# The last two token blocks of a PEER layer: both whole expert tables multiplied on TensorE in place of gathers

## Chip, core and metric

The kernel runs on one core of a Trainium2 chip. The metric is the device time of one execution in microseconds (us). The 16 DMA engines of the core, the GpSimd queue that issues gathers (POOL), SyncE's queue of plain transfers (SP), TensorE (PE), VectorE (DVE) and ScalarE (ACT) all take part.

## What is computed

One residual layer on 1024 tokens of width 1024: a token mixer (convolution branch, stick-breaking attention branch, gates, output projection, LayerNorm) and then a channel mixer, PEER, in blocks of 128 tokens. Only PEER is touched by the change:

```python
def block(xb):                                   # 128 tokens
    q = (xb @ w_q).reshape(128, 8, 2, 128)
    s1, s2 = einsum('thd,hkd->thk', q[:, :, 0], k1), einsum(..., q[:, :, 1], k2)
    v1, i1 = top_k(s1, 16);  v2, i2 = top_k(s2, 16)
    top_s, pos = top_k(v1[..., :, None] + v2[..., None, :], 16)   # of 256 pairs
    idx = i1 * 128 + i2 at pos                   # one of 16384 experts
    gate = softmax(top_s)
    act = gelu(einsum('td,thkd->thk', xb, expert_u[idx]))
    return einsum('thk,thkd->td', gate * act, expert_v[idx])
x = layer_norm(alpha * x + PEER(x))
```

All is float32. A token of a head picks 16 experts, so a block of 128 tokens needs 8 x 16 = 128 pairs of rows (u, v) per token.

## The kernel before, in words

The token mixer of the second half of the sequence (four blocks) is done first. Then one long run of **turns** does PEER: one turn is one head of one block, 8 blocks x 8 heads = 64 turns (`TURNS`), and a turn has 8 **steps** (`STEPS`). A step handles two of the 16 picked experts per token. Blocks 4 to 7 of the turns are the first half of the sequence; their token mixer (late convolution, late attention, late mixing) is spread over the steps of turns 1 to 31 by hand, in `beside(t, g)`.

In a step (turn t, step g) this happens:
- POOL gathers, for each of the two experts, 128 rows of the joined table `uv` (8 KB each: u and v) into one of `RING` = 8 slots (L727; a slot is free when `experts` of four steps earlier is done).
- DVE takes the dot product of x1 with the u half (`dots`, L2033), then a part of the top-k of a later turn (`pick`), then the part of `beside`.
- ACT does the gelu, the product with the gate and two small diagonal matrices (L1480, L1482, L1489).
- PE multiplies the diagonals with the v half, 16 matmuls of 32x32 by 512 columns (`experts`, L1002), in PSUM banks 0 to 3 (4 to 7 for odd late blocks, `y_bank`).

Every engine runs its own list in the order of the steps, so what an engine waits for in a step also holds up what it has to do in the next. The scores of the late blocks for one head ("slab") are made in turns 30 to 38 (`slab_in_turn`); the last slab is scored in turn 38. At the end of a block `merge`, `y_out` and `finish` normalise it and SP stores it.

A float32 matmul stands in the trace as two instructions. The three matmuls of `split_products` (L256 to L258) are the other way that this kernel multiplies: each operand is cut in a rounded fp32r part (made by ACT) and a rest (made by DVE), and each of the three products is one instruction.

Of the kernel before, what the change touches and what calls it, by code (L numbers as in the profile page):

```python
# [29 lines left out]
P = 128  # L30
# [49 lines left out]

def wait_alone(eng, sem, value, started):


    value = eng.to_reg(value)
    eng.wait_ge(started, 1)
    eng.wait_ge(sem, value)
# [5 lines left out]
TURNS = NB * PH  # L92
# [89 lines left out]
def build(nc, xT_d, x_d, w_proj_d, w_v_d, w_mix_d, w_out_d, slabs_d, uv_d, cols_d, bv_d,  # L182
          b_out_d, ln1_g_d, ln1_b_d, ln2_g_d, ln2_b_d, out_d):
    ctx = ExitStack()
    with ctx:  # L185
# [22 lines left out]
        x_lo_bytes = overlay("x_lo_bytes", 160, 176, F32R)  # L208
        ctx.enter_context(nc.sbuf_tensor("arenas", [P, HIGH * KB], F32))
# [113 lines left out]

        def small(name, shape, dt=F32):
            return ctx.enter_context(nc.sbuf_tensor(name, [P] + shape, dt))
# [19 lines left out]
        iota_i = small("iota_i", [TOPK], mybir.dt.int32)  # L345
        top_s = small("top_s", [TOPK])
# [131 lines left out]

        block = ctx.enter_context(nc.Block())
# [10 lines left out]
        def y_bank(pb):  # L490
            return 4 if pb > BLK and pb % 2 == 1 else 0
# [17 lines left out]
        def _(sp_eng):  # L509
# [164 lines left out]
            for pb in range(BLK, NB - 1):  # L674
                store_out(pb)
            for half in range(2):
                hs = slice(half * HALF, (half + 1) * HALF)
                sp_eng.wait_ge(out_ready, NB + half)
                sp_eng.dma_start(out_d[row_of(NB - 1):row_of(NB - 1) + P, hs], pre2[:, hs]).then_inc(stored, 16)
            sp_eng.wait_ge(stored, 16 * (NB + 1))  # L680
# [3 lines left out]
        def _(pool):  # L684
# [7 lines left out]
            pool.memset(quad_eye, 0.0).then_inc(pool_step, 1)  # L692
            pool.iota(iota_i[:, :], pattern=[[1, TOPK]], base=0, channel_multiplier=0).then_inc(consts, 1)
# [40 lines left out]
        def _(pe):  # L734
# [272 lines left out]
            def banks_free(pb):  # L1007
                if pb <= BLK and pb >= 1:
                    pe.wait_ge(y_read, pb)
                if pb == BLK + 1:  # L1010
                    pe.wait_ge(score_ready, len(SLABS))
                if pb > BLK + 1:
                    pe.wait_ge(y_read, pb - 1)
# [211 lines left out]

            def select(t, g):
# [30 lines left out]
            for t in range(TURNS):  # L1257
                for g in range(STEPS):
                    if t % PH == 0 and 1 <= t // PH <= BLK and g == 0:
                        merge(t // PH - 1)  # L1260
                    if t % PH == 0 and t // PH > BLK and g == 1:
                        merge(t // PH - 1)
# [18 lines left out]
        def _(act):  # L1281
# [342 lines left out]

            def select(t, g):
# [51 lines left out]
            for t in range(TURNS):  # L1677
                act.wait_ge(gates_ready, t + 1)
                steps = Steps(act, gelu_step, t * TOPK)
                for g in range(STEPS):  # L1680
                    if t % PH == 0 and 1 <= t // PH <= BLK and g == 0:
                        odd_out(t // PH - 1)
# [8 lines left out]
                    if t % PH == 0 and t // PH > BLK and g == 0:  # L1691
                        odd_out(t // PH - 1)
# [4 lines left out]
                    for n in rows_at(t * STEPS + g):  # L1697
                        spread_out(n)
                    if t == 0 and g in (1, 6):
                        std1(2 + g // 4)  # L1700
                assert steps.n == TOPK
            odd_out(NB - 1)
            finish_std(NB - 1)
# [3 lines left out]
        def _(dve):  # L1707
# [249 lines left out]
            dve.wait_ge(consts, 6)  # L1957
            nc.vector.tensor_copy(iota16[:, :], iota_i[:, :]).then_inc(iota_ready, 1)
# [86 lines left out]
            def finish(pb, part):  # L2045
# [8 lines left out]
                if part == 3 and pb + 1 < NB:  # L2054
                    norm_scale(pre2, pre2, ln2_b_bc).then_inc(out_ready, 1)
                if part == 3 and pb + 1 == NB:
                    for half in range(2):
                        hs = slice(half * HALF, (half + 1) * HALF)
                        norm_scale(pre2[:, hs], pre2[:, hs], ln2_b_bc[:, hs]).then_inc(out_ready, 1)
# [142 lines left out]
            next_steps = Steps(dve, topk_step, FIRST_STEPS)  # L2202
            for t in range(TURNS):
                steps, next_steps = next_steps, Steps(dve, topk_step, FIRST_STEPS + (t + 1) * TOPK_STEPS)
                for g in range(STEPS):
                    dots(t, g)
                    if t % PH == 0 and t >= 1 and g == (1 if t // PH > BLK else 0):
# [17 lines left out]
                    beside(t, g)  # L2225
                assert t + 1 == TURNS or steps.n == TOPK_STEPS
            y_out(NB - 1)
            for part in range(4):
                finish(NB - 1, part)
# [57 lines left out]
```

## Time and profile before

| | us |
|---|---|
| median of 3 runs | 3086.72 (3085.66 to 3087.18) |
| the profiled execution, span | 3085.0 |
| PE busy | 2081.4 (67%) |
| DVE busy | 2314.1 (75%) |
| ACT busy | 1153.7 (37%) |
| POOL busy | 1339.0 (43%) |
| moved by DMA | 1172.07 MB, of it 1073.81 MB by the gathers' queue |

The page gives the span in 40 slices of 77 us: tenths of an engine's busy time, the TensorE clock granted (in tenths of 2.4 GHz), the mean busy share of the 16 DMA engines and the GB/s moved. A wait is given as idle time of the engine ahead of a group of instructions, with who ended it. The profiled span is 1.7 us under the median.

### The profile page before, as it was taken

The page shows a single profiled execution, that of the slowest core. Times are in us where ns is not written, and L with a number is a line of the kernel's source. Part 1 is how long each engine was busy: PE and PEld are TensorE (multiplying, and loading weights), DVE is VectorE, ACT ScalarE, POOL GpSimd, SP SyncE. Part 2 cuts the span into 40 slices and gives each one's busy share as a digit, 9 for nine tenths or more (in the row PEclk, how much of TensorE's full clock was granted, in tenths as well). Part 3 has the DMA queues.
Part 4 walks back from the last instruction along what each step waited for, and adds up shares of the span by engine and source line. Part 5 has one row for each costly group of instructions (what it writes and reads, how often), then busy time and mean ns, then how long its engine had stood idle before and what let it go on. Part 6 is the DMA issues. An engine that isn't in the chain of part 4 may idle for free. (4 is left out here: it accounts for less than half of the span.)

```text
span 3085.0 us, 54203 instructions
## 1 busy us (share of the span) xinstructions
PE 2081.4 (67%) x20660; PEld 830.9 (27%) x20660; DVE 2314.1 (75%) x4890; ACT 1153.7 (37%) x3376; POOL 1339.0 (43%) x1175
## 2 busy tenths in 40 slices
PE   9999878787987777678889767654344434443443
PEld 7777433232323333323323222210000000000000
DVE  7965678999789898967668766667776767677764
ACT  3353243333445455534334343333333333333222
POOL 0000244444445555633434444445555555555553
PEclk9999989888987877789989888875555555555555
DMA  4113799999999999999999999999999999999997
GB/s 163 60 64 137 275 413 405 419 416 409 415 421 417 419 417 420 417 421 421 419 420 410 420 421 421 419 419 419 418 419 418 418 420 419 417 417 419 417 419 303
DMA packets 167847, 1172.07 MB, mean 380 GB/s; under 512 B 18357, under 2 KB 18485, under 8 KB 31034
## 3 DMA queue, kind: packets, MB, share of 16 engines
q0 software_dynamic: 147456, 1073.81, 84.1%
q1 hardware_dynamic: 20154, 95.01, 7.9%
q8 instruction: 160, 2.62, 0.3%
q14 instruction: 77, 0.63, 0.1%
HBM read 1164.55 MB, written 4.19 MB: 379 GB/s over the span
## 5 line engine op out<-in xcount | busy, mean ns | idle before, releaser
L727 POOL DMA_INDIRECT arena_high<-uv_dram,idx_now x1024 | 1273.4, 1244 | 1381.9 <-PE ps L1002 1196.2
L2033 DVE SCALAR_TENSOR_TENSOR arena_high<-arena_low,arena_high 128x1024 f32<-128x1024 f32 x1024 | 1242.2, 1224 | 581.1 <-DMA arena_high<-uv_dram,idx_now 572.3
L1002 PE MATMUL ps<-arena_high 32*32 32x512 f32 x16384 | 820.5, 835 | 937.3 <-ACT arena_high L1489 933.3
L1480 ACT ACTIVATE gcol<-hcol 128x2 f32<-128x2 f32 x512 | 104.0, 203 | 1581.6 <-DVE arena_high L2033 1581.3
L1002 PEld LDWEIGHTS ps<-arena_high 32*32 32x32 f32 x16384 | 136.6, 119 | 1483.0 <-ACT arena_high L1489 1402.9
L1489 ACT ACTIVATE arena_high<-arena_high,wcol 128x32 f32<-128x32 f32 x1024 | 272.9, 313 | 16.7
L963 PE MATMUL ps<-arena_low 128*128 128x512 f32 (+1 forms) x512 | 253.2, 637 | 0.2 <-issue 0.2
L1482 ACT ACTIVATE wcol<-gcol,arena_high 128x1 f32<-128x1 f32 x1024 | 245.6, 287 | 16.9
L722 POOL CAST idx_now<-arena_high 128x8 uint32<-128x8 f32 x128 | 62.4, 488 | 209.1 <-DVE arena_high L2019 208.6
L963 PEld LDWEIGHTS ps<-arena_low 128*128 128x128 f32 x512 | 101.9, 213 | 168.8 <-issue 159.2
L1141 PE MATMUL ps<-arena_low 128*128 128x512 f32 x256 | 126.0, 638 | 0.0
L256 PE MATMUL ps<-x_hi_bytes,w_hi_bytes 128*128 128x512 f32 x256 | 104.1, 407 | 7.2 <-DVE x_lo_bytes L1720 7.2
L1480 ACT ACT_TABLE_LOAD x79 | 101.4, 1283 | 6.1 <-DVE arena_high L2033 4.8
L257 PE MATMUL ps<-x_lo_bytes,w_hi_bytes 128*128 128x512 f32 x256 | 101.4, 396 | 0.0
L258 PE MATMUL ps<-x_hi_bytes,w_bytes 128*128 128x512 f32 x256 | 101.2, 395 | 0.0
L1738 DVE SCALAR_TENSOR_TENSOR arena_low<-arena_low,cols 128x512 f32<-128x512 f32 x120 | 90.0, 750 | 2.8
L2033 DVE DVE_READ_ACCUMULATOR arena_high<-arena_low,arena_high 128x1 f32 x1024 | 84.3, 82 | 0.0
L1474 ACT ACT_TABLE_LOAD x64 | 82.1, 1283 | 1.1
L1970 DVE MAX8 arena_high<-arena_high 128x8 f32<-128x128 f32 x256 | 74.2, 290 | 6.1 <-ACT arena_high L1670 5.0
L1125 PE MATMUL ps<-arena_low 128*64 128x128 f32 x416 | 72.3, 343 | 1.2 <-ACT arena_low L1562 1.2
L1971 DVE FIND_INDEX8 top_i<-arena_high 128x8 uint32<-128x128 f32 x256 | 72.8, 284 | 0.0
L1125 PEld LDWEIGHTS ps<-arena_low 128*64 128x64 f32 x416 | 63.4, 180 | 29.2 <-issue 18.0
(207 smaller groups left out, 2546.9 us busy)
## 6 DMA issues: line engine op xcount, KB each, us to landing
arena_low<-slabs_dram SPq DMA_DIRECT2D x20, 1152.0 KB, 10.0
arena_high<-uv_dram,idx_now POOLq DMA_INDIRECT x1024, 12.5
arena_low<-w_mix_dram SPq DMA_DIRECT2D x8, 1536.0 KB, 11.5
arena_high<-w_proj_dram SPq DMA_DIRECT2D x16, 512.0 KB, 3.2
arena_high<-w_mix_dram SPq DMA_DIRECT2D x8, 1024.0 KB, 5.0
arena_low<-w_proj_dram SPq DMA_DIRECT2D x16, 512.0 KB, 11.7
arena_high<-w_mix_dram SPq DMA_DIRECT2D x8, 512.0 KB, 7.0
arena_high<-w_out_dram SPq DMA_DIRECT2D x2, 2048.0 KB, 9.6
```

The source lines that it names most:

```text
L256: nc.tensor.matmul(out, w_hi, x_hi, start=first, stop=False)
L257: nc.tensor.matmul(out, w_hi, x_lo, start=False, stop=False)
L258: return nc.tensor.matmul(out, w_lo, x_hi, start=False, stop=last)
L727: pool.indirect_dma_start(out=ring[:, s % RING, :], out_offset=None, in_=uv_d, in_offset=bass.IndirectOffsetOnAxis(ap=idx_now[:, s:s + 1], ...
L963: last = nc.tensor.matmul(ps[:, 4 + half, j0 * P:j1 * P], w[:, k, half * P:(half + 1) * P], x1T[:, j0:j1, k, :], start=(k == 0), stop=(k = ...
L1002: last = nc.tensor.matmul(ps[out:out + QUAD, y_bank(t // PH) + turn, :], diag[rows, s % DIAGS, :], ring[rows, s % RING, cs], start=fresh, ...
L1125: last = nc.tensor.matmul(ps[r, 7, b * P:(b + 1) * P], v_block(b + m)[:, p * P + hd * DH:p * P + (hd + 1) * DH], kq_late[:, hd, m, :], sta ...
L1141: last = nc.tensor.matmul(ps[:, 4 + g, :], w_mix_late[m % 2][:, o:o + P], xT_late[:, k, :], start=(k == 0), stop=(k == KD - 1))
L1480: steps.link(nc.scalar.activation(gcol[:, s0:s0 + 2], hcol[:, s0:s0 + 2], ACT.Gelu))
L1482: last = nc.scalar.activation(wcol[:, s:s + 1], gcol[:, s:s + 1], ACT.Copy, scale=gates[:, t % (BLK * PH), s:s + 1])
L1489: nc.scalar.activation(diag[:, s % DIAGS, :], quad_eye, ACT.Copy, scale=wcol[:, s:s + 1]).then_inc(diag_ready, 1)
L2033: last = nc.vector.scalar_tensor_tensor(out=ring[:, s % RING, 0:D], in0=x1[c][:, j, :], scalar=1.0, in1=ring[:, s % RING, 0:D], op0=ALU.mu ...
```

## The change

`DENSE` = 2: the last two blocks (6 and 7) leave the turns, `TURNS` is 48. Their PEER is done as dense products with all 16384 experts, beside the steps of turns 39 to 47 (`U0` = 39 x 8 is the first step, 72 steps up to the last):

1. **Picks.** From turn 32 on, one part of a pick of the two blocks per step (`dense_pick`, 16 picks of 5 parts, 80 steps) on DVE, its exponential on ACT. They leave, per token and head, both key numbers and the gate in `picks`.
2. **First table, 41 steps.** u is given transposed, as 128 tiles of 128 experts x 1024 (`ut`). SP loads each (512 KB, 8 slots), PE multiplies it with the 256 tokens (`u_tile`, 8 float32 matmuls of 128x128 by 256 columns), ACT takes the gelu of two tiles at a time (`dense_act`) and SP stores the result in DRAM (`act_d`, 16 chunks of 1 MB).
3. **Gates spread, 16 of these steps** (from the 25th). For groups of four tokens DVE makes one-hot matrices from `picks` (`hot_group`, 8 instructions of 128x128), PE multiplies them (`g_group`, 4 float32 matmuls of 128 columns): the 128 x 128 gates of each token. ACT copies, SP stores (`g_d`, 16 MB in all).
4. **Second table, 31 steps.** SP loads a chunk of gates (1 MB, read in pieces of 512 B) and of activations (1 MB) for 8 tiles and the tiles of v (512 KB, 4 slots). DVE multiplies the chunk (128x2048), ACT rounds it, DVE makes the rest. Of each v tile ACT makes the rounded part, DVE the rest, and PE does `v_tile`: 2 blocks x 2 halves x 3 = 12 matmuls of 512 columns in banks 4 to 7.
5. **End.** `dense_finish` normalises the two blocks one after the other, after the last gathered block.

The merge of all blocks is in banks 0 to 3 (`y_bank` is 0). The diff, cut:

```diff
+DENSE = 2
+GB = NB - DENSE
+TURNS = GB * PH
...
+U0 = 39 * 8
+U_STEPS, V_STEPS = 41, 31
+PICK0 = 32 * 8
+PICK_PARTS = 5
+NT = NKEY
+CH = 8
+GROUPS = DENSE * P // 4
+G_STEP0 = 24
+def u_first(s):
+    return NT * s // U_STEPS
+def v_first(v):
+    return NT * v // V_STEPS
+def w_step(c):
+    return U_STEPS + max(v for v in range(V_STEPS) if v_first(v) <= c * CH) - 1
...
 @block.sync
+            def load_u(n):
+                if n == 0:
+                    sp_eng.wait_ge(score_psum, len(SLABS))
+                if n >= 8:
+                    wait_again(sp_eng, u_used, n - 7)
+                sp_eng.dma_start(u_slot[n % 8].rearrange("p a b -> p (a b)"), ut_d[n, :, :]).then_inc(u_in[n % 8].sem, 16)
+            def load_v(n):
+                if n < 4:
+                    wait_again(sp_eng, u_used, NT - 7 + n)
+                else:
+                    wait_again(sp_eng, v_used, n - 3)
+                sp_eng.dma_start(v_raw[n % 4], uv_d[n * P:(n + 1) * P, D:2 * D]).then_inc(v_in[n % 4].sem, 16)
+            def load_chunk(c):
+                if c == 0:
+                    for i in range(2):
+                        wait_again(sp_eng, act_stored[i], 16 * NT // CH // 2)
+                        wait_again(sp_eng, g_stored[i], 16 * 16 // 2)
+                if c >= 2:
+                    wait_again(sp_eng, v_used, CH * (c - 1))
+                src = g_d[:, :, c * CH * 16:(c + 1) * CH * 16].rearrange("a p b -> p a b")
+                sp_eng.dma_start(g_in[c % 2], src).then_inc(chunk_in[c % 2].sem, 16)
+                sp_eng.dma_start(act_in[c % 2].rearrange("p a b -> p (a b)"), act_d[c, :, :]).then_inc(chunk_in[c % 2].sem, 16)
...
+            for n in range(4, NT):
+                if n % CH == 4 and CH < n < NT - CH:
+                    load_chunk(n // CH + 1)
+                load_v(n)
...
 @block.tensor
+            def u_tile(n):
+                if n >= 4 and n % 2 == 0:
+                    wait_again(pe, act_ready, n // 2 - 1)
+                wait_again(pe, u_in[n % 8], 16 * (n // 8 + 1))
+                for k in range(KD):
+                    last = nc.tensor.matmul(ps[:, 4 + n % 4 // 2, o:o + 2 * P], u_slot[n % 8][:, k, :],
+                                            x1T[:, BLK - DENSE:BLK, k, :], ...)
+            def g_group(i):
+                wait_again(pe, hot_ready, i + 1)
+                if i >= 2:
+                    wait_again(pe, g_read, i - 1)
+                for q in range(4):
+                    last = nc.tensor.matmul(ps[:, 6 + i % 2, q * P:(q + 1) * P], hot[:, i % 2, q, 0:P],
+                                            hot[:, i % 2, q, P:2 * P], start=True, stop=True, ...)
+            def v_tile(n):
+                if n % CH == 0:
+                    wait_again(pe, w_low, n // CH + 1)
+                wait_again(pe, v_lo_done, n + 1)
+                for j in range(DENSE):
+                    for h in range(2):
+                        last = split_products(ps[:, 4 + 2 * j + h, :], (w_hi_c[...], w_lo_c[...]),
+                                              (v_hi_r[n % 4][:, hs], v_lo_r[n % 4][:, hs]), n == 0, n == NT - 1)
...
+                    dense(t * STEPS + g - U0)
                     experts(t, g)
-            merge(NB - 1)
+            merge(GB - 1)
...
 @block.vector
+            def dense(G):
+                k, part = divmod(G - PICK0, PICK_PARTS)
+                if 0 <= k < DENSE * PH:
+                    dense_pick(k, part, pick_steps)
+                s = G - U0
+                if G_STEP0 <= s < G_STEP0 + 16:
+                    for i in range(4 * (s - G_STEP0), 4 * (s - G_STEP0) + 4):
+                        hot_group(i)
+                now = [c for c in range(NT // CH) if s == w_step(c)]
+                for c in now:
+                    wait_again(dve, chunk_in[c % 2], 32 * (c // 2 + 1))
+                    nc.vector.tensor_tensor(a, a, g_in[...], ALU.mult).then_inc(w_mul.sem, 1)
+                v = s - U_STEPS
+                if -1 <= v < V_STEPS:
+                    for n in range(v_first(v) + 2 if v >= 0 else 0, min(v_first(v + 1) + 2, NT)):
+                        wait_again(dve, v_rounded, n + 1)
+                        nc.vector.tensor_tensor(v_lo_r[n % 4], v_raw[n % 4], v_hi_r[n % 4].bitcast(F32), ALU.subtract)
+                for c in now:
+                    wait_again(dve, w_high, c + 1)
+                    nc.vector.tensor_tensor(w_lo_c[c % 2], act_in[c % 2], w_hi_c[c % 2].bitcast(F32), ALU.subtract)
...
```

`wait_again` waits on a semaphore of an earlier stage that is used a second time. ACT's list has the roundings (`round_v`, the chunk's `w_hi_c`) behind its work for the experts of the same step.

How the lists change at three places. In these rows a float32 matmul counts once. PE, before, from the last scores of turn 38 on (L963 and L987 are the last queries and scores, L1002 the experts, L1025 the merges):

```order
L963 MATMUL ps<-arena_low 128x384 x4
L1002 MATMUL ps<-arena_high 32x512 x16
L987 MATMUL ps<-arena_low 128x128 x6
L1002 MATMUL ps<-arena_high 32x512 x160
L1025 MATMUL ps<-arena_high 32x512 x12
L1002 MATMUL ps<-arena_high 32x512 x1024
```

PE, changed, the same place and then, behind the "...", where the spreading of the gates begins (L1152 is `experts`, L1389 `u_tile`, L1377 the transposed picks, L1402 `g_group`):

```order
L1137 MATMUL ps<-arena_low 128x128 x6
L1152 MATMUL ps<-arena_high 32x512 x16
L1389 MATMUL ps<-arena_low 128x256 x24
L1152 MATMUL ps<-arena_high 32x512 x16
...
L1377 MATMUL ps<-arena_high,arena_low 128x128 x6
L1389 MATMUL ps<-arena_low 128x256 x32
L1402 MATMUL ps<-arena_low 128x128 x16
L1152 MATMUL ps<-arena_high 32x512 x16
```

Each step's 16 expert matmuls now stand behind three or four tiles of u, and in 16 steps also behind four groups.

DVE, changed, two steps of the second table (L2299 is `dots`, L2405 the product of a chunk, L2411 the rest of a v tile, L2415 the rest of a chunk; L2266 and L2270 belong to a pick):

```order
L2299 SCALAR_TENSOR_TENSOR arena_high,hcol<-arena_low,arena_high 128x1024 x2
L2266 TENSOR_TENSOR arena_high<-arena_high,top_i 128x512
L2270 TENSOR_REDUCE arena_high<-arena_high 128x16
L2405 TENSOR_TENSOR arena_low<-arena_low 128x2048
L2411 TENSOR_TENSOR x_hi_bytes<-arena_low,wv_hi_bytes 128x1024 x4
L2415 TENSOR_TENSOR w_lo_bytes<-arena_low,w_hi_bytes 128x2048
L2299 SCALAR_TENSOR_TENSOR arena_high,hcol<-arena_low,arena_high 128x1024 x2
L2411 TENSOR_TENSOR x_hi_bytes<-arena_low,wv_hi_bytes 128x1024 x4
```

Before, only the dots and the picks stood there. The dots of a step are now behind the four rests of the step ahead.

## Rows read from the trace of the kernel before

**Rows 1.** The page: the span in 40 slices (tenths)

```profile
DMA  4113799999999999999999999999999999999997
...
q0 software_dynamic: 147456, 1073.81, 84.1%
```

**Rows 2.** Stages: window, PE, PEld, DVE, ACT, POOL busy (instructions), PEclk, DMA share, GB/s

```profile
1763.00:2059.00 296.00, 198.62 (x2092) 70.77 (x2092) 200.93 (x480) 102.18 (x336) 132.49 (x123) 0.83 1.01 420
2059.00:3069.00 1010.00, 410.26 (x6472) 60.74 (x6472) 704.93 (x1621) 325.80 (x1114) 526.43 (x444) 0.51 1.00 416
```

**Rows 3.** DVE at L2033 alone up to a time (two instructions per dot product)

```profile
0.00:2059.00 2059.00, 756.67 (x1248) 0.88 0.89 365
```

**Rows 4.** Group of DVE in 2059 to 3069: busy us, mean ns, idle before, releaser

```profile
L2033 DVE SCALAR_TENSOR_TENSOR arena_high<-arena_low,arena_high 128x1024 f32<-128x1024 f32 x400 | 489.4, 1224 | 284.8 <-DMA arena_high<-uv_dram,idx_now 281.4
```

**Rows 5.** Groups of DVE in 1763 to 2059

```profile
L2033 DVE SCALAR_TENSOR_TENSOR arena_high<-arena_low,arena_high 128x1024 f32<-128x1024 f32 x110 | 133.7, 1223 | 89.9 <-DMA arena_high<-uv_dram,idx_now 89.5
...
L2033 DVE DVE_READ_ACCUMULATOR arena_high<-arena_low,arena_high 128x1 f32 x110 | 9.1, 82 | 0.0
```

**Rows 6.** PE in order of time: start us, us, what, [idle before]

```profile
572.19 3.70 PE L963 MATMUL ps<-arena_low 128*128 128x512 f32 x8
575.82 1.14 PE L1002 MATMUL ps<-arena_high 32*32 32x512 f32 x32
576.89 2.05 PE L987 MATMUL ps<-arena_low 128*128 128x128 f32 x16
...
1812.95 2.02 PE L1002 MATMUL ps<-arena_high 32*32 32x512 f32 x32 [5.47 <-ACT arena_high L1489]
1814.90 4.68 PE L963 MATMUL ps<-arena_low 128*128 128x512 f32 x6
1819.52 1.14 PE L1002 MATMUL ps<-arena_high 32*32 32x512 f32 x32
1820.59 2.84 PE L963 MATMUL ps<-arena_low 128*128 128x512 f32 x6
```

**Rows 7.** PE in order of time, split products of the projections

```profile
59.65 0.39 PE L256 MATMUL ps<-x_hi_bytes,w_hi_bytes 128*128 128x512 f32 x1
...
65.77 0.39 PE L256 MATMUL ps<-x_hi_bytes,w_hi_bytes 128*128 128x512 f32 x1
```

**Rows 8.** Groups of ACT and DVE over the whole span

```profile
L1562 ACT ACTIVATE arena_low<-ps 128x512 f32<-128x512 f32 x40 | 23.0, 576 | 0.0
L1284 ACT ACTIVATE w_hi_bytes<-arena_high 128x1024 fp32r<-128x1024 f32 x16 | 17.0, 1062 | 41.2 <-DMA arena_high<-w_proj_dram 41.2
...
L1714 DVE TENSOR_TENSOR w_bytes<-arena_high,w_hi_bytes 128x1024 fp32r<-128x1024 f32 x16 | 19.6, 1225 | 6.1 <-ACT w_hi_bytes L1284 5.5
L2103 DVE COPY arena_low<-arena_high 128x128 f32<-128x128 f32 x1 | 0.2, 221 | 0.0
```

**Rows 9.** ACT's work for one step, in order of time

```profile
2301.65 0.20 ACT L1480 ACTIVATE gcol<-hcol 128x2 f32<-128x2 f32 x1 [3.69 <-DVE arena_high L2033]
...
2302.40 0.53 ACT L1489 ACTIVATE arena_high<-arena_high,wcol 128x32 f32<-128x32 f32 x2
```

**Rows 10.** Transfers by line: KB each, median us from issue to landing

```profile
arena_low<-slabs_dram SPq DMA_DIRECT2D x20, 1152.0 KB, 10.0
...
arena_high<-w_proj_dram SPq DMA_DIRECT2D x16, 512.0 KB, 3.2
...
arena_high<-x_dram SPq DMA_DIRECT2D x8, 512.0 KB, 8.0
...
out_dram<-arena_high SPq DMA_DIRECT2D x7, 512.0 KB, 9.1
```

**Rows 11.** The end: PE, then DVE, in order of time

```profile
3069.46 2.02 PE L1002 MATMUL ps<-arena_high 32*32 32x512 f32 x32 [2.88 <-ACT arena_high L1489]
...
3076.86 1.22 DVE L2042 SCALAR_TENSOR_TENSOR arena_high<-arena_low,ps 128x1024 f32<-128x1024 f32 x1 [8.76 <-PE ps L1025]
...
3081.07 1.42 DVE L1904 SCALAR_TENSOR_TENSOR arena_high<-arena_high,rstd 128x512 f32<-128x512 f32 x2
```

More of the change, by code:

```diff
@@ L477, in build @@
         rows_spread = sem("rows_spread")
+        u_in = [Again(xT_in[i], 32 if i < PAIRS else 16) for i in range(8)]
+        u_used = Again(z_done, 32)
+        act_ready = Again(rest_done, 32)
+        act_stored = [Again(wout_in[i], 16) for i in range(2)]
+        d_step = Again(beta_done, 32)
+        d_shifted = Again(stick_done, 32)
+        d_exp = Again(att_done, 32)
+        picked = Again(turned, 32)
+        picks_turned = Again(v_done, 4)
+        picks_ready = Again(v_read, 4)
+        hot_ready = Again(att_kq_done, 32)
+        g_psum = Again(av_done, 16)
+        g_read = Again(out_read, 4)
+        g_stored = [Again(wv_in, 16), Again(bv_in, 16)]
+        v_in = [Again(wbranch_in[i], 32) for i in range(4)]
+        v_rounded = Again(gates_done, 16)
+        v_lo_done = Again(sigs_ready, 16)
+        v_used = Again(branch_done, 8)
+        chunk_in = [Again(wconv_in[i], 64) for i in range(2)]
+        w_mul = Again(mix_step, 8)
+        w_high = Again(w_rounded, 24)
+        w_low = Again(w_split, 24)
         block = ctx.enter_context(nc.Block())
@@ new lines, in _ @@
+            for n in range(NT):
+                load_u(n)
+                if n % CH == 0 and n >= 2 * CH:
+                    store_act(n // CH - 2)
+                for i in range(16):
+                    if n == u_first(G_STEP0 + i + 1) + 8:
+                        store_g(i)
+                if n == u_first(17) + 8:
+                    store_out(BLK)
+            store_act(NT // CH - 2)
+            for i in range(16):
+                if u_first(G_STEP0 + i + 1) + 8 >= NT:
+                    store_g(i)
@@ new lines, in _ @@
+            for n in range(4):
+                load_v(n)
+            store_act(NT // CH - 1)
+            load_chunk(0)
+            load_chunk(1)
+            for n in range(4, NT):
+                if n % CH == 4 and CH < n < NT - CH:
+                    load_chunk(n // CH + 1)
+                load_v(n)
+            store_out(GB - 1)
+            for j in range(DENSE):
+                sp_eng.wait_ge(out_ready, GB + 1 + j)
+                sp_eng.dma_start(out_d[row_of(GB + j):row_of(GB + j) + P, :], dense_y[j]).then_inc(stored, 16)
@@ L683, in _ @@
+            sp_eng.wait_ge(stored, 16 * NB)
         @block.gpsimd
@@ L1698, in _ @@
                         spread_out(n)
+                    dense(t * STEPS + g)
                     if t == 0 and g in (1, 6):
@@ L1701, in _ @@
                 assert steps.n == TOPK
-            odd_out(NB - 1)
-            finish_std(NB - 1)
+            odd_out(GB - 1)
+            for pb in range(GB - 1, NB):
+                finish_std(pb)
         @block.vector
@@ new lines, in hot_group @@
+            def hot_group(i):
+                if i == 0:
+                    wait_again(dve, picks_ready, 1)
+                if i >= 2:
+                    wait_again(dve, g_psum, i - 1)
+                j = i // (P // 4)
+                for q in range(4):
+                    t = 4 * i + q - j * P
+                    nc.vector.tensor_scalar(hot[:, i % 2, q, 0:P], iota128[:, :], picksT[:, j, 1, t:t + 1], None, ALU.is_equal)
+                    last = nc.vector.tensor_scalar(hot[:, i % 2, q, P:2 * P], iota128[:, :], picksT[:, j, 0, t:t + 1],
+                                                   picksT[:, j, 2, t:t + 1], ALU.is_equal, ALU.mult)
+                last.then_inc(hot_ready.sem, 1)
@@ L2225, in _ @@
                     beside(t, g)
+                    dense(t * STEPS + g)
                 assert t + 1 == TURNS or steps.n == TOPK_STEPS
-            y_out(NB - 1)
+            y_out(GB - 1)
             for part in range(4):
-                finish(NB - 1, part)
+                finish(GB - 1, part)
+            for j in range(DENSE):
+                dense_finish(j)
 def kernel(x, w_in, b_in, conv_w_dw, conv_b_dw, conv_ln_g, conv_ln_b, conv_w_pw2, conv_b_pw2, sb_w_o,
```

225 lines of the change are left out of this document (196 added, 29 removed).

## The prediction, before the changed kernel was run

> **What bounds the kernel now.** I read the page's slices first: from about 400 us to the end the 16 DMA engines are busy throughout, and 84.1% of their time over the span is the gathers' queue [rows 1]. Then the stages [rows 2]: in the last 1010 us, from turn 39 on, the DMA share is 1.00 at 416 GB/s while PE is busy 410 us, DVE 705, ACT 326. Then who waits: DVE sat idle 281 us there for gathers [rows 4]. So each step costs what its 2 MB of gathered rows cost, 1010 / 200 steps = 5.05 us; only fewer bytes, or nothing, makes this stage shorter. Turn 39 begins at 2059 us: 39 x 16 = 624 dot products, 1248 instructions, are done by then [rows 3].
>
> In bytes the change is a gain. It takes away 256 gathers of 1.05 MB, 268 MB, and adds 134 MB of tables and four times 16.8 MB of gates and activations written and read again, 201 MB. That is 67 MB less, 160 us at 420 GB/s, if bytes were still the limit. They are not: the work moves to PE, so the sum is made stage by stage. The 25 turns from 39 on become 9.
>
> **Part 1, up to turn 39.** A pick costs DVE, in turns 32 to 38, its busy time less dots less one normalisation: 200.9 [rows 2] - 133.7 - 9.1 [rows 5] - 5.6 [rows 11] = 52.5 us for 7 turns, 7.5 us each, some 8.3 with the gaps between its linked instructions. The 56 steps of these turns get 56 parts of 5, 11.2 picks: 93 us. DVE's idle time for gathers there is 89.5 us [rows 5]. So the picks fill DVE to the brim while DMA is also full. Bounds: 4 us (idle time used to the last) to 30 (a third is lost, since a heavy part in one step can't use the idle time of another beyond the four steps of the ring). I take 15. Turn 39 starts at 2074. The other picks (24 steps) fall in steps that PE makes long: nothing.
>
> **Part 2, first table, 41 steps.** On a warm PE 8 instructions of 512 columns take from 572.19 to 575.82 [rows 6], of which some 0.2 is the change of shape: 0.43 each. A float32 matmul is two, 256 columns half as long: 0.215 per instruction, 16 per tile, 128 tiles: 440 us. Shape changes 41 x 0.2 = 8. The experts of a step take 1.07 (575.82 to 576.89 [rows 6]): 44. Together 492, 12.0 us a step. DMA there moves 2.1 + 1.6 + 0.8 MB per step, 10.8 us at 420 GB/s: it lies beside PE, and with eight slots a late tile has 28 us of cover. The gelu (0.58 per pair of tiles [rows 8]) is beside it too. The gates: a group is 8 instructions of 128 columns, 0.128 each (16 in 2.05 us [rows 6]), 1.03 us on PE. DVE's eight one-hots cost some 8 x 0.22 = 1.8 us by the nearest row, a copy of 128x128 [rows 8]. With two buffers, two groups of a step are ready and two come at DVE's pace: 2 x 1.03 + 2 x 1.9 = 5.8 us in each of 16 steps (bounds 4.1 by PE alone, 7.6 by DVE alone): 93 us. The first tile lands 8 us after the last scores [rows 10] with 1 us of experts beside it, and the picks are turned and copied before the first group (3 us): 10. Sum 595; bounds 568 and 625.
>
> **Part 3, between the tables.** The first chunk is not loaded before the last activations are stored, and DVE and ACT stand in front of it: gelu 0.6 [rows 8], store 9.1, load 10.0 (1152 KB, by [rows 10]; it is 2 MB in all, read in short pieces), product of 2048 columns 2.4, rounding 2.0, rest 2.4 (twice the rows of 1024 [rows 8]): 26.5, less the experts beside it: 25 us. Bounds 18 (transfers as quick as the 3.2 us row) and 35.
>
> **Part 4, second table, 31 steps.** A split product goes every 0.2267 us (27 in 65.77 - 59.65 = 6.12 [rows 7]): 12 per tile 2.72 us, 4.13 tiles per step 11.2, with shape change and experts 12.5 us. Were PE never late, 388 us. But v has four slots, and a tile holds its slot from its load until PE has used it. Call a step's tiles a, b, c, d. DVE leaves a step only after the rest of the next step's b, whose slot came free when PE finished this b, 5.4 us into the step. It lands L later; rounding 1.06 and rest 1.23 [rows 8] end at 7.7 + L. Then come two dots, 2.6, and ACT's work for the experts, 1.3 [rows 9], which stands ahead of its roundings: next c is rounded at 7.7 + L + 2.6 + 1.3 + 1.1 and its rest is done at 13.9 + L. PE wants it 5.4 us into a step of length X. With c late by s each time, X = 12.5 + s and 13.9 + L = X + 5.4 + s, so s = (L - 4.0) / 2. L is 8.0 beside saturated gathers and 3.2 in the early stage with DMA a quarter busy (512 KB [rows 10]). Here DMA would be some 80% busy; I take 6: s = 1.0. Every second step has a chunk: its product (2.4) stands ahead of c and the wait for ACT's rounding and the rest adds 3.2 behind b; by the same halving (2.4 + 3.2) / 4 = 1.4 per step. The chunk's 2.1 MB are queued on SP ahead of four tiles, 5 us at 420 GB/s, in half of the steps, halved: 1.2. X = 12.5 + 1.0 + 1.4 + 1.2 = 16.1, 499 us. Bounds: 388, and X = 20, 620 us (L = 8, 17.1, and PE falls to the lower clock after each wait: after 5.47 us idle the same experts took 2.02 and the six matmuls 4.68 in place of 1.14 and 2.84 [rows 6], 2.7 us).
>
> One rule bears on L. The Trainium skill, "DMA: Bandwidth & Descriptors", section "Anatomy of one DMA — SWDGE (gpsimd) path", fits a transfer as 2.0 us + bytes / 436e3; for a v tile that is 3.2 us, an estimate, with which s is zero. The 3.2 us row of the early stage agrees, the 8.0 row beside gathers doesn't, and by the rule alone the sum would be rival B's, about 3110.
>
> **Part 5, the end.** From the last experts to the end 3085 - 3071.5 = 13.5 us [rows 11]. Two more normalisations follow on DVE, from 3076.86 to 3082.5 one takes 5.6, with gaps 6: 12. A whole row block stored in place of a half: 1. 26 us.
>
> **Sum**: 2074 + 595 + 25 + 499 + 26 = 3219 of span, and the median stood 1.7 us above the profiled span: 3221 us, 4.3% slower. The merges between turns cost nothing new: PE has u tiles to do behind them.
>
> **Rivals.**
> - *B, second table without stalls.* The gathers no longer saturate DMA, tiles land in 3 to 4 us, and PE is the only limit. 3219 - 499 + 388 = 3108, 3110 us; up to 3150 with a few stalls. For it: 5.3 MB per step are 12.7 us at 420 GB/s, so bytes alone would allow it. Against: DVE's own work in a step is 2.6 + 0.9 + 5.1 + 2.4 = 11 of 12.5 us with two waits in the middle.
> - *C, faster.* PE is the bound and every cover holds: the picks fit in DVE's idle time (2059), groups go at PE's pace (568), the transfers between the tables are quick (18), no stalls (388), end 22. 3055 + 2 = 3057, 1.0% faster. It decides at Part 4: with the other terms at these ends X may be 13.4 us, with the terms I took no X at all gives a gain. Against it: it needs all five ends.
> - *D, the clock and the queue.* X = 20 with PE cold after each wait and chunks late: 3219 + 121 = 3340, 3342 us. For it: PE's granted clock was 0.83 already where it was two thirds busy [rows 2].
> - *The picks don't hide* (30 in place of 15) only adds 15 to any of these.
>
> **How the numbers follow.** The forecast case, X from 14.5 to 18, 3170 to 3280 us: 0.55. B (3100 to 3170): 0.20. D (over 3280): 0.13. C and what lies between it and B: 0.12. The predicted time is 3221. The range takes in B and most of D: 3100 to 3335, with C's 0.12 and some 0.08 of D outside. A change of 0.2% (6 us) is about what this measurement can tell. Faster by more: 0.09, within: 0.03, slower: 0.88.
>
> **What would show it.** Right: PE over 90% busy at a clock of 1.0 from turn 39 through the first table, steps of 12 us and 17 to 18 us with gates; an idle stretch of about 25 us on PE and DVE between the tables; then steps of about 16 us, PE idle for DVE's rests (L2411, L2415) at 3 to 4 us a step, DMA no longer saturated, gathers waiting for slots. Turn 39 beginning 10 to 30 us later than before, DVE busy without a gap. Wrong: a first pass longer than 625 us, a second below 420, DMA share still near 1 in either, or fewer PE cycles per tile than its rows give.

## Result and profile after

| | us |
|---|---|
| before, beside the changed kernel | 3086.95 (3085.66 to 3089.92, 4 runs) |
| changed kernel | 3270.66 (3261.34 to 3283.26, 4 runs) |
| ratio | 1.0597, 95% interval 1.0571 to 1.0622 |
| predicted | 3221, range 3100 to 3335, slower with 0.88 |

The change costs 184 us. The profiled execution took 3261.3 us (span 3259.5), the quickest of the four, so the sum below is made against 3259.5. One of the five executions of e2 below ran at a granted clock of 0.551 from its first microsecond to its last, near the lower level of 1.2 GHz, and took 4350 us; the time of e2 leaves it out.

The page of the changed kernel, the same views as [rows 1], with PE and its clock:

```profile
PE   9999888878976777798896666899999877777886
DVE  8864769999798989676687999744355646555655
PEclk9999998889967777899898888899999998889998
DMA  4114899999999999999999999989978777778884
...
q0 software_dynamic: 110592, 805.36, 61.3%
q1 hardware_dynamic: 96810, 296.36, 24.3%
```

DMA is full up to slice 26, where turn 39 begins, as before, and then no longer: the gathers' queue fell by 268 MB, the plain one rose by 201 MB. PE is the full one in the slices of the first table, and nobody is in those of the second. The stages from the first tile of u on (first table, the stretch between the tables, second table, end; columns as in [rows 2]):

```profile
2076.50:2675.30 598.80, 569.39 (x3870) 462.08 (x3870) 301.64 (x999) 154.48 (x372) 83.88 (x90) 0.99 0.85 315
2675.30:2699.60 24.30, 1.38 (x34) 0.37 (x33) 7.16 (x5) 4.40 (x4) 1.89 (x2) 0.62 0.91 309
2699.60:3234.90 535.30, 431.58 (x2496) 315.84 (x2496) 310.22 (x360) 201.21 (x308) 78.62 (x60) 0.91 0.79 283
3234.90:3259.50 24.60, 3.50 (x57) 0.72 (x56) 15.90 (x21) 3.68 (x6) 0.00 (x0) 0.69 0.16 64
```

Before, the same work was the single stage of 1010 us of [rows 2], with DMA at 1.00 and PE at half clock. Turn 39 begins at 2070 us (the count of [rows 3]):

```profile
0.00:2070.00 2070.00, 752.98 (x1248) 0.88 0.89 364
```

Who waited in the second table, all engines (us in total, times, longest):

```profile
POOL arena_high L877 <- PE ps L1152: 410.9, 27, 35.5
ACT wv_hi_bytes L1859 <- DMA arena_low<-uv_dram: 208.6, 70, 10.6
DVE x_hi_bytes L2411 <- ACT wv_hi_bytes L1859: 177.2, 68, 10.3
...
PE ps L298 <- DVE x_hi_bytes L2411: 95.0, 31, 9.1
...
DVE arena_low L2405 <- DMA arena_low<-acts_dram: 32.7, 8, 9.2
PE ps L298 <- DVE w_lo_bytes L2415: 31.4, 5, 22.9
```

This is to be read from below. PE waits for a rest (95 us); DVE, who makes it, for the rounding (177); ACT for the tile of v to land (209). The gathers, which had held up everybody before, wait 411 us for a free slot. One step of it, in order of time, from its second dot at 2899.28 (L2299) on; SP's loads of the next tiles begin at 2900.37:

```profile
2899.28 1.22 DVE L2299 SCALAR_TENSOR_TENSOR arena_high<-arena_low,arena_high 128x1024 f32<-128x1024 f32 x1
...
2900.37 7.16 SPq L789 DMA_DIRECT2D arena_low<-uv_dram  x3
...
2902.87 2.36 DVE L2411 TENSOR_TENSOR x_hi_bytes<-arena_low,wv_hi_bytes 128x1024 fp32r<-128x1024 f32 x2 [1.37 <-ACT wv_hi_bytes L1859]
...
2904.15 0.50 PE L298 MATMUL ps<-wv_hi_bytes,w_hi_bytes 128*128 128x512 f32 x1 [1.09 <-DVE x_hi_bytes L2411]
...
2907.55 1.06 ACT L1859 ACTIVATE wv_hi_bytes<-arena_low 128x1024 fp32r<-128x1024 f32 x1 [3.83 <-DMA arena_low<-uv_dram]
...
2911.87 1.06 ACT L1859 ACTIVATE wv_hi_bytes<-arena_low 128x1024 fp32r<-128x1024 f32 x1 [3.26 <-DMA arena_low<-uv_dram]
...
2914.10 1.22 DVE L2299 SCALAR_TENSOR_TENSOR arena_high<-arena_low,arena_high 128x1024 f32<-128x1024 f32 x1
```

The first dot of the next step (2914.10) comes right behind the rest whose tile landed at 2911.87. DVE did nothing from 2909.9 to 2913.0, though the dots need nothing of v.

### The profile page after: what moved, and what is told of

Same layout as the page of the kernel before. It is cut to its first block and busy times, and to the rows that moved or that the text cites. A ratio compares the mean times of both kernels' runs of the same rounds, so it can differ in the third digit from the quotient of the medians.

```text
span 3259.5 us, 53459 instructions
## 1 busy us (share of the span) xinstructions
PE 2687.0 (82%) x20618; PEld 1549.5 (48%) x20618; DVE 2338.0 (72%) x5034; ACT 1218.0 (37%) x2996; POOL 990.5 (30%) x888
## 5 line engine op out<-in xcount | busy, mean ns | idle before, releaser
L877 POOL DMA_INDIRECT arena_high<-uv_dram,idx_now x768 | 947.2, 1233 | 1853.9 <-PE ps L1152 1707.5
L2299 DVE SCALAR_TENSOR_TENSOR arena_high<-arena_low,arena_high 128x1024 f32<-128x1024 f32 x768 | 920.8, 1223 | 261.1 <-DMA arena_high<-uv_dram,idx_now 255.7
L1152 PE MATMUL ps<-arena_high 32*32 32x512 f32 x12288 | 511.3, 695 | 341.4 <-ACT arena_high L1700 337.4
L1389 PE MATMUL ps<-arena_low 128*128 128x256 f32 x2048 | 455.1, 382 | 5.9 <-DMA arena_low<-ut_dram 5.9
L1389 PEld LDWEIGHTS ps<-arena_low 128*128 128x128 f32 x2048 | 387.4, 191 | 94.0 <-issue 34.3
L1152 PEld LDWEIGHTS ps<-arena_high 32*32 32x32 f32 x12288 | 95.2, 109 | 566.8 <-ACT arena_high L1700 481.3
L298 PE MATMUL ps<-wv_hi_bytes,w_hi_bytes 128*128 128x512 f32 x512 | 220.7, 431 | 126.6 <-DVE x_hi_bytes L2411 95.0
L2411 DVE TENSOR_TENSOR x_hi_bytes<-arena_low,wv_hi_bytes 128x1024 fp32r<-128x1024 f32 x128 | 153.7, 1224 | 178.0 <-ACT wv_hi_bytes L1859 177.2
L299 PE MATMUL ps<-x_hi_bytes,w_hi_bytes 128*128 128x512 f32 x512 | 213.7, 417 | 0.0
L300 PE MATMUL ps<-wv_hi_bytes,w_lo_bytes 128*128 128x512 f32 x512 | 212.7, 415 | 0.0
L1859 ACT ACTIVATE wv_hi_bytes<-arena_low 128x1024 fp32r<-128x1024 f32 x128 | 132.3, 1053 | 208.9 <-DMA arena_low<-uv_dram 208.6
L1700 ACT ACTIVATE arena_high<-arena_high,wcol 128x32 f32<-128x32 f32 x768 | 204.9, 314 | 12.5
L1113 PEld LDWEIGHTS ps<-arena_low 128*128 128x128 f32 x512 | 103.9, 217 | 173.8 <-issue 162.3
## 6 DMA issues: line engine op xcount, KB each, us to landing
spread_dram<-arena_high SPq DMA_DIRECT2D x16, 1024.0 KB, 10.5
```

Source lines behind the costliest of these rows:

```text
L298: nc.tensor.matmul(out, w_hi, x_hi, start=first, stop=False)
L299: nc.tensor.matmul(out, w_hi, x_lo, start=False, stop=False)
L300: return nc.tensor.matmul(out, w_lo, x_hi, start=False, stop=last)
L877: pool.indirect_dma_start(out=ring[:, s % RING, :], out_offset=None, in_=uv_d, in_offset=bass.IndirectOffsetOnAxis(ap=idx_now[:, s:s + 1], ...
L1113: last = nc.tensor.matmul(ps[:, 4 + half, j0 * P:j1 * P], w[:, k, half * P:(half + 1) * P], x1T[:, j0:j1, k, :], start=(k == 0), stop=(k = ...
L1152: last = nc.tensor.matmul(ps[out:out + QUAD, y_bank(t // PH) + turn, :], diag[rows, s % DIAGS, :], ring[rows, s % RING, cs], start=fresh, ...
```

## Experiments

The theory: on PE's path lie, besides its own work, (a) in the second table the loop of a v slot (four slots; load, rounding, rest, product) with all engines bound to the order of steps, (b) in the first one-hots built too late for PE, (c) between the tables the chain store, load, product, rounding, rest, (d) before turn 39 DVE filled by picks. The rival for all of it: the transfers themselves. Times in us, medians of four runs beside the kernel before on the same chip; the ratio of the changed kernel is 1.0597, and 0.001 of it is 3.1 us. The changed kernel's median stands 9 us above its profiled run, so most gains by medians come out 4 to 14 us larger than the same gains between the profiled spans.

| kernel | time | ratio to before (95%) |
|---|---|---|
| e1 six slots | 3221.9 | 1.0438 (1.0420 to 1.0456) |
| e2 groups between tiles | 3225.1 | 1.0440 (1.0422 to 1.0458) |
| e3 early chunk | 3254.8 | 1.0556 (1.0526 to 1.0586) |
| e4 second table in float32 | 3206.7 | 1.0381 (1.0362 to 1.0399) |
| e5 no gate chunks | 3240.5 | 1.0495 (1.0475 to 1.0514) |
| e6 = e1 + e2 + e3 | 3178.8 | 1.0295 (1.0276 to 1.0315) |
| e7 = e6, product behind | 3208.3 | 1.0398 (1.0380 to 1.0415) |
| e8 = e4 + e2 + e3 | 3157.1 | 1.0228 (1.0211 to 1.0245) |
| e9 half the searches | 3260.1 | 1.0556 (1.0538 to 1.0573) |
| e10 = e6, three ahead | 3169.0 | 1.0255 (1.0229 to 1.0281) |
| e11 = e8, half the u products (2 runs) | 3060.8 | 0.9914 (0.9881 to 0.9948) |

What e2 changes in the trace is read in e6.

**e1, two more slots.** In the 16 KB that the stored gates leave free in the second table:

```diff
-        v_raw = [at(64 + 4 * i, D) for i in range(4)]
+        v_raw = [at(64 + 4 * i, D) for i in range(4)] + [at(176 + 4 * i, D) for i in range(2)]
...
-                else:
-                    wait_again(sp_eng, v_used, n - 3)
+                elif n >= SLOTS:
+                    wait_again(sp_eng, v_used, n - SLOTS + 1)
```

> Two more slots for tiles of v (six in place of four), nothing else. Theory (the slot loop: a tile of v is loaded only when PE has finished the tile four before it, so DVE leaves each step late): a tile's slot comes free two tiles, 5.4 us, earlier, L - 9.4 is negative, and PE's idle time for DVE's rests (95 us in the changed kernel) falls to about 30; the second table takes 420 to 450 us in place of 535, the whole 3150 to 3180. Rival 1 (the transfers themselves: short pieces, chunks and tiles on one queue): the DMA share of 0.79 stays, the second table keeps 510 to 535 us. Rival 2 (DVE's own work of 11 us a step in the way): less than 20 us gained.

Measured: 49 us less. The second table took 493 us in place of 535 (first split product at 2698.5, last at 3191.1), and PE waits for the rests of v in two rows now:

```profile
PE ps L300 <- DVE x_hi_bytes L2413: 49.9, 15, 6.1
...
PE ps L300 <- DVE v_more_bytes L2413: 14.5, 8, 2.6
```

64 us in place of 95, not 30. So the loop is real, the size was not: I had expected 420 to 450 us for the stage. Neither rival holds (the DMA share rose to 0.83, the stage lost 42 us), but some two thirds of the stalls stay with six slots.

**e5, no chunks of gates.** The second half of a chunk, all its short pieces, is not loaded from the third chunk on:

```diff
+                if c < 2:
                     sp_eng.dma_start(g_in[c % 2], src).then_inc(chunk_in[c % 2].sem, 16)
```

> Left out: the loads of the chunks of gates from the third chunk on (14 MB, all of it in pieces of 512 B); the products use the gates of the first two chunks again. Theory (a chunk costs by standing on SP's queue ahead of four tiles of v, 1.2 us a step for 2 MB, so half of that for 1 MB): the second table is 15 to 25 us shorter than 535. Rival 1 (short pieces are what slows DMA there): 50 us or more. Rival 2 (only the slot loop counts): under 8 us.

Measured: the ratio falls by 0.0102, 31 us; the second table took 510 us, 25 less, at the upper end of the theory's band and far below the rival's. The page's packets give the price of short pieces apart from the queue, in the second table of the changed kernel:

```profile
q1 hardware_dynamic: 48768, 94.38, 50.5%
q0 software_dynamic: 7776, 56.63, 27.9%
```

1.87 MB per percent of DMA time for SP's queue against 2.03 for the gathers': 9% dearer for all that queue, short pieces included. That leaves the chunk's place ahead of four tiles of v, and one thing more. The transfer of activations is issued right behind that of the gates, and issuing it holds SP (min/median/max in ns; changed kernel, then e5):

```profile
L801 SPq DMA_DIRECT2D arena_low<-acts_dram x16: 3634/5174/6808, 2680.6 to 3177.7; - x16
...
L802 SPq DMA_DIRECT2D arena_low<-acts_dram x16: 431/432/5717, 2683.4 to 3155.5; - x16
```

5.2 us in the median, 0.43 where no gates are loaded ahead of it, and the tiles of v behind it can't be issued meanwhile. e5 takes the bytes, the place in the queue and this hold away together; which of them makes the 25 us is not shown.

**e7, the chunk's product behind the rests**, and **e10, three tiles ahead**, both on e6:

```diff
-                for c in now:
-                    wait_again(dve, chunk_in[c % 2], 32 * (c // 2 + 1))
-                    ...
                 v = s - U_STEPS
...
+                for c in now:
+                    wait_again(dve, chunk_in[c % 2], 32 * (c // 2 + 1))
+                    ...
                 for c in now:
                     wait_again(dve, w_high, c + 1)
```

> As e6, and DVE's product of a chunk stands behind the step's rests of v tiles in place of ahead of them. Theory (with six slots DVE waits 50 to 80 us for a chunk's activations with the rests of four tiles behind it): 20 to 40 us less than e6. Rival (ACT's rounding and the rest of the chunk then come too late for PE): same as e6 or slower.

```diff
-                    for n in range(v_first(v) + 2 if v >= 0 else 0, min(v_first(v + 1) + 2, NT)):
+                    for n in range(v_first(v) + 3 if v >= 0 else 0, min(v_first(v + 1) + 3, NT)):
```

> As e6 (six slots, groups between tiles, early chunk), with ACT and DVE three v tiles ahead of the step's end in place of two. Theory (what is left of PE's 66 us of waits for rests in e6 is DVE and ACT starting a step's third tile too late, behind dots and a chunk's product): 20 to 40 us less than e6, 3140 to 3160. Rival (a tile further ahead ties DVE to a slot that is freed one tile later, as in the changed kernel, and the dots of the next step wait for it): no gain or a loss.

Measured: e7 is 29 us slower than e6 (second table 520 us against 493): the rival. DVE's wait for the chunk went from its list, 48 us, but it then waited 28 us for the rounding of the chunk (7 in e6) and 161 for the roundings of v (114 in e6), which ACT does in the same order as before. e10 is 10 us quicker than e6 by the medians, but the intervals overlap; its second table took 484 us in place of 493. That is the theory's direction at half the least it had asked for.

**e4, the second table in float32.** No roundings, no rests, tiles read from eight slots:

```diff
-                        last = split_products(ps[:, 4 + 2 * j + h, :], (w_hi_c[...], w_lo_c[...]),
-                                              (v_hi_r[n % 4][:, hs], v_lo_r[n % 4][:, hs]), n == 0, n == NT - 1)
+                        last = nc.tensor.matmul(ps[:, 4 + 2 * j + h, :], act_in[c % 2][:, i, js], v_raw[n % 8][:, hs],
+                                                start=(n == 0), stop=(n == NT - 1))
```

> Second table in float32 without splitting: eight slots, no roundings and no rests on ACT and DVE, 4 float32 matmuls (8 instructions) of 512 columns per tile, 3.44 us in place of 2.72. Theory (slot loop and DVE's and ACT's steps are what costs 17.3 us a step, PE itself only 12.5): PE becomes the bound at 15.5 us a step, 480 us in place of 535, in spite of a fourth more PE work; whole 3195 to 3215. Rival 1 (transfers limit the second table): 535 stays. Rival 2 (PE work counts in full): 535 + 92 = 627 us, slower than the changed kernel.

Measured: 67 us less. The second table ran from 2705.3 to 3184 us, 479, and PE waited for nothing in it but at its start:

```profile
2705.30:3184.00 478.70, 478.68 (x1983) 199.60 (x1984) 126.08 (x219) 46.33 (x167) 60.75 (x60) 1.00 0.84 318
```

A fourth more PE work, the same bytes, and a shorter stage: both rivals fall. Of the 147 us over the 388 that PE needs at full clock, the 56 down to 479 are shown to come from roundings, rests and four slots, and not from a limit of the transfers. Whether the transfers would allow less than 479 no run shows; the stage's 151 MB at the 411 GB/s of e11 are 368 us, an estimate. e4 changes the slots and the helpers' work together, so it doesn't part them.

**e2, groups between the tiles.** On PE, and the same on ACT:

```diff
                     for n in range(u_first(s), u_first(s + 1)):
                         u_tile(n)
-                if G_STEP0 <= s < G_STEP0 + 16:
-                    for i in range(4 * (s - G_STEP0), 4 * (s - G_STEP0) + 4):
-                        g_group(i)
+                        if left:
+                            g_group(left.pop(0))
+                for i in left:
+                    g_group(i)
```

> First table: one group of gates behind each u tile on PE (and the copies on ACT in the same order) in place of four groups behind the step's tiles. Theory (PE's 62 us of idle time ahead of groups is DVE building one-hots at 2.1 us a group with two buffers, and u tiles can cover it): idle goes to under 10, the first table takes 540 in place of 599 us, the whole 3205 to 3215. Rival (the first table is limited by transfers or by DVE's total work in these steps): PE's idle time moves to another wait and less than 20 us are gained.

Measured: 48 us less. The 62 us of that expectation were a misreading: the view by line adds PE's and its weight load's idle time. By engine it is 28 us, in the first table of the changed kernel, and gone in e6. Two steps of the changed kernel:

```profile
2457.11 1.16 PE L1402 MATMUL ps<-arena_low 128*128 128x128 f32 x8 [1.10 <-DVE arena_low L2388]
2458.92 1.77 PE L1402 MATMUL ps<-arena_low 128*128 128x128 f32 x8 [0.65 <-DVE arena_low L2388]
2460.63 2.01 PE L1152 MATMUL ps<-arena_high 32*32 32x512 f32 x32
2462.57 10.67 PE L1389 MATMUL ps<-arena_low 128*128 128x256 f32 x48
2473.08 1.95 PE L1402 MATMUL ps<-arena_low 128*128 128x128 f32 x16
2476.12 1.16 PE L1402 MATMUL ps<-arena_low 128*128 128x128 f32 x8 [1.10 <-DVE arena_low L2388]
2477.93 1.16 PE L1402 MATMUL ps<-arena_low 128*128 128x128 f32 x8 [0.65 <-DVE arena_low L2388]
2479.02 1.14 PE L1152 MATMUL ps<-arena_high 32*32 32x512 f32 x32
2480.10 5.23 PE L1389 MATMUL ps<-arena_low 128*128 128x256 f32 x23
```

After waits of 1.1 and 0.65 us the same eight instructions took 1.77 in place of 1.16 and the experts 2.01 in place of 1.14: the granted clock fell. A step later the same two waits left it at its full level. Of the 16 steps with groups, all with these waits, it fell in four (at 2387, 2458, 2534 and 2623 us), at 1.5 us each. In e6 and e8 the first table took 556 us (2082.6 to 2639.4 and 2081.4 to 2637.0) in place of 599. Of these 43 us, 28 are waits and some 6 the clock. The remaining 9 are PE's own pace: the step from 2462.57 to 2480.10 takes 17.53 us at full clock with 1.75 of waits, the same instructions with a group behind each tile 15.20 in e8:

```profile
2407.02 3.72 PE L1390 MATMUL ps<-arena_low 128*128 128x256 f32 x16
2410.58 1.05 PE L1403 MATMUL ps<-arena_low 128*128 128x128 f32 x8
...
2421.15 1.14 PE L1153 MATMUL ps<-arena_high 32*32 32x512 f32 x32
2422.22 1.13 PE L1390 MATMUL ps<-arena_low 128*128 128x256 f32 x4
```

**e3, the first chunk earlier.**

```diff
-                if c == 0:
-                    for i in range(2):
-                        wait_again(sp_eng, act_stored[i], 16 * NT // CH // 2)
+                if c < 2:
+                    wait_again(sp_eng, act_stored[c], 16 * NT // CH // 2)
...
-            store_act(NT // CH - 1)
             load_chunk(0)
+            store_act(NT // CH - 1)
             load_chunk(1)
```

> The first chunk is loaded before the last activations are stored (it needs only the stores of its own buffer and of the gates). Theory (the 24 us between the tables are a chain store, load, product, rounding, rest): PE's idle stretch of 22.9 us shrinks by the last store's share, to 8 to 14, and the whole is 9 to 14 us shorter. Rival (the stretch is set by the tiles of v or by ACT's order): no change.

Measured: 0.0041 of the ratio, 13 us, with intervals that overlap; in the trace PE's idle stretch went from 22.9 to 16.1 us, a little above the band. The chain is right, the last store was 7 us of it.

**e6 and e8, together.**

> Six slots, groups between the tiles and the early chunk in one kernel. Theory (three separate waits on PE's path, which add): 49 + 48 + 13 = 110 us less than the changed kernel, a ratio of 1.024 to before, 3160 us. Rival (the first two share a limit, or the early chunk's gain was the slots' one too): 3175 us or more.

> Second table in float32 with eight slots (e4), with groups between the tiles and the early chunk. Theory (the gains add, PE is the bound in both tables): 67 + 48 + 7 to 13 us less than the changed kernel, 3140 to 3150 us, PE without idle time over 10 us from turn 39 on but for the stretch between the tables. Rival (an undisturbed PE is held up elsewhere: activations, picks, transfers): 3165 us or more.

Measured: e6 is 92 us under the changed kernel where the three gains make 110; turn 39 began some 6 us later in it, for a reason I have not found, and its second table took 493 us as in e1. The 110 is a sum of three gains by medians, each taken from the changed kernel's high median. In the traces the gains do add: 43 in the first table, 42 in the second and 7 between them, less the 6, are 86, and the profiled spans differ by 85. e8 is 114 us under the changed kernel, where the sum is 122 to 128. The stages of e8:

```profile
2081.40:2637.20 555.80, 554.46 (x3870) 456.88 (x3870) 302.32 (x998) 153.18 (x372) 82.92 (x90) 1.00 0.91 339
2649.90:3130.00 480.10, 480.10 (x1997) 199.96 (x2007) 126.07 (x219) 46.34 (x167) 63.64 (x60) 1.00 0.85 321
```

PE is busy all the time at full clock, and still the kernel is 2.3% slower than before. So in this form the tables lose without a stall: 556 + 480 = 1036 us of PE work stand where 1010 us of gathers stood. That is 26 of the 69 us by which the profiled spans differ; the others are turn 39's later start and the first tile (22), the stretch between the tables (13) and the end (8). In the split form it is otherwise. With 388 us in place of 480 for the second table, e8's span of 3154 would be 3062, under the 3085 of before. That is an estimate: no run had the split products without waits.

**e11, half of the u products left out**, on e8:

```diff
-                for k in range(KD):
+                for k in range(KD // 2):
```

> On e8 (second table in float32, groups between tiles, early chunk). Left out: the last four of the eight products of each u tile, 220 us of PE's work; all transfers stay. If PE alone bounds the first table in e8 (PE busy 554 of 556 us there): it shrinks by 220 us to 335. Theory: bytes are close behind, some 186 MB at the 420 GB/s of the kernel before are 443 us, so it shrinks to 440 to 460 us with a DMA share over 0.98, and the whole to 3040 to 3060, under the kernel before. Rival (gathers and loads hinder each other and no 420 GB/s are reached in this mixture, as 339 GB/s in e8): 500 us or more.

Measured: 3060.8 us, faster than before. The first table took 449 us (2076.3 to 2524.9), and its stretch reads:

```profile
2081.00:2536.00 455.00, 356.50 (x2867) 265.23 (x2865) 299.17 (x992) 152.24 (x373) 87.74 (x92) 0.95 1.01 411
```

That is the theory: bytes, at 411 GB/s, are the next bound in the first table, 107 us below PE's. It does only half of the first product and is no version of the kernel.

**e9, half the searches.**

```diff
-                if part < 2:
+                if part < 2 and k % 2 == 0:
...
-                    for i in range(2):
+                    for i in range(0 if k % 2 else 2):
```

> Left out: the top-k searches of the last block's eight heads (they take over what the other block found), two thirds of the work of 8 of the 16 added picks. Theory (the picks fill DVE in turns 32 to 38 and push turn 39 from 2059 to 2070): some 37 us less work for DVE in these turns, DVE waits for gathers again, turn 39 begins at 2059 to 2062, the whole 8 to 11 us shorter. Rival (the later start of turn 39 has another cause, or DVE's load there doesn't matter): turn 39 still begins at 2070, the whole within 3 us.

Measured: DVE is busy 258.8 us of the 296 of [rows 2] in place of 282.5 and waits 25.9 us for gathers again, but turn 39 begins only some 3 us earlier. So the searches are a part of the 11 us, and where the rest comes from stays open; the other half of the picks was still there. The whole is 0.0041 of the ratio, 13 us, under the changed kernel; the profiled spans differ by 3.5 us (3259.5 and 3256.0), which those 3 us explain, and the rest comes in with the changed kernel's high median.

## Why the prediction was right, and where not

| term | predicted | measured |
|---|---|---|
| turn 39 begins | 2074 | 2070 |
| first table, with its start | 595 | 605 |
| between the tables | 25 | 24 |
| second table | 499 | 535 |
| end | 26 | 25 |
| span | 3219 | 3259.5 |

- *What bounds the kernel.* The stage's bound moved from DMA to PE as described; 67 MB fewer are moved, at 0.85 and 0.79 of DMA's time. Shown by e8, in float32: with nearly every wait of PE taken away but the one between the tables it is slower than before. The split form without a wait was reached by no run; the best, e10, is 2.5% slower than before. The signs named for the second table came: PE idle for rests at 3.3 us a step (104 / 31), gathers waiting for slots.
- *Part 1.* DVE without a gap in turns 32 to 38 (282.5 of 296 us busy, no wait for gathers), turn 39 later by 11 where I took 15. By e9 that reason is only a part of it.
- *Part 2.* The rows for PE held: 48 instructions of u took 10.5 us (2462.57 to 2473.08), 0.219 each where I had 0.215. The groups' 5.8 us were measured as 5.9 (2473.08 to 2479.02). The waits there, 28 us, were in the sum as 16 x (5.8 - 4.1) = 27. The first tile came after 6.5 us where the sum had 10. What the sum lacked is some 8 us of lower clock, 2 at the first tiles (2076.53) and 6 in four of the steps with groups, and 4 for a merge (L1171), which it had put at nothing.
- *Part 3.* The chain and its size were right; a part of 7 us could be cut (e3).
- *Part 4* is the step that was sized too small: X = 17.3 us a step in place of 16.1. I took L = 6 and the tiles landed in a median of 6.2 us. PE's waits in the stage are 126.6 - 22.9 = 104 us, where the sum had (16.1 - 12.5) x 31 = 112. The missing 36 us are the clock: PE was busy 432 us in the stage for work of 388, granted 0.91. By the starts of its split products, 0.43 us apart in place of 0.227, PE ran at the lower level 18 times, for 2.7 to 6.1 us each, which cost some 35 us. Each time a wait of 1.8 to 9.1 us stood ahead (22.9 at the stage's start), while some waits up to 3.3 us left the clock full. I had put a price on that in rival D alone.
- *The same step by its parts.* The sum's 112 us of waits were 31 for the slot loop, 43 for the chunk's product and 37 for the queue. With six slots the equation leaves no stall of the loop (L - 9.4, s = 0), so 31 of PE's waits should go and 80 stay. e1 took 40 away and left 64, near both. It was e1's own expectation, 30 us left, that asked more of the slots than the sum had given them. L is no constant either: with six slots the tiles in the old slots landed after 9.5 us in the median, in place of 6.2; I take it that they are issued earlier and stand behind more, which no run shows. e5 puts a chunk's gates at 25 us of the stage where the sum had half of 1.2 x 31 = 19. The share of the chunk's product was measured by no run: e7 moved it and lost. That the waits agree in total (104 and 112) is in part luck, since that term and the halvings behind it are untested.
- *The rule on a transfer's time.* The fit of the Trainium skill's page "DMA: Bandwidth & Descriptors", section "Anatomy of one DMA — SWDGE (gpsimd) path", would give 3.2 us per tile, an estimate. It is a fit for single transfers of gpsimd's queue, and the tiles go by SP's. The trace has 6.2 beside the gathers with DMA at 0.79. Rival B, which hung on tiles landing in 3 to 4 us, did not come.
- *Rival C.* It needed all its ends at once. Two of the five were reached, and only by edits: groups at PE's pace (e6 and e8), and an idle stretch between the tables of 16.3 us in e6 and 11.5 in e8, under the 18. Turn 39 never began at 2059, the end took 24 to 25 us and the split products never ran without a wait.
- *The median* stands 9 us above the profiled run, where it was 1.7 before: the changed kernel varies by 0.7%, the kernel before by 0.1%. Why was not tried.

## What to carry to other kernels

Fewer bytes are a gain only as long as bytes stay the bound: before work is moved from a full DMA to an engine that looks idle, add up that engine's new work at full clock against the time that the bytes take now (here 492 + 66 + 388 = 946 us of PE against 1010 us of gathers), and see what is left for the rest: 10 at the start, 25 between the tables and 12 more at the end left 17 us for all waits of 72 steps and the clock they cost, 11 of which went with turn 39's later start. The waits and what came with them took 147 in the second table and 41 in the first. Where each tile is loaded, rounded, subtracted and multiplied on four in-order lists, price the waits and the clock that PE loses behind them (here 35 us on 104 of waits); a float32 product with a fourth more PE work and none of the helpers was 56 us quicker in that stage. And put small matmuls that depend on another engine between the large ones rather than behind them: 43 us for a change of order alone.

## What was not expected of the hardware

- PE's granted clock can fall after short waits, and not every time. In the changed kernel waits of 1.1 and 0.65 us came in 16 steps, and in four of them it fell (the eight instructions of 1.77 in place of 1.16 us), though PE was fully busy on both sides. In the second table it stayed full after a wait of 3.3 us and fell after one of 1.8. In e8, without waits, it was 1.00 in both tables.
- A transfer can be dear for the queue that issues the next one: behind a load of 1 MB in pieces of 512 B, SP was held 5.2 us in issuing, and 0.43 without it (e5).
